# A decoder trunk on one core: gate products and first projection of the gated-delta stage in eight blocks, three weight pieces split before the stage, convolution rows loaded and turned before its norm

## The chip, the core and the metric

The kernel runs on one core of a Trainium2 chip. The metric is the device time of one execution in microseconds (us). Five engines work side by side, each with its own instruction queue: TensorE (PE, with PEld for its weight loads), VectorE (DVE), ScalarE (ACT), GpSimd (POOL) and SyncE (SP), which here only starts DMAs. They are ordered by semaphores alone: an instruction that waits holds up all that stands behind it on its engine.

## The reference

The program is one inference step of a four-layer decoder for 256 prompt tokens and 32 sample tokens (8 sequences of 4). Tokens lie side by side, so an activation is 1024 features by 288 tokens. Each layer is half an FFN, a token mixer and half an FFN, all behind an RMSNorm:

```
x = x + 1/2 * FFN_a(RMSNorm(x));  x = x + Mixer(RMSNorm(x));  x = x + 1/2 * FFN_b(RMSNorm(x))
```

The mixers of the layers are RWKV-7, differential attention, gated DeltaNet and RWKV-7. The change is in the entry of the gated DeltaNet (third layer):

```
proj = u @ p['w_in']                       # u = RMSNorm(x); 1024 -> 3072 (q|k|v) + 1024 (z) + 8 (b) + 8 (a)
xp = concatenate([conv_prev, qkv], axis=1) # 3 rows of state per sequence
conv = sum(p['conv_w'][j] * xp[:, j:j + T] for j in range(4))
qkv_c = silu(conv)
beta = sigmoid(b_raw);  g = -exp(a_log) * softplus(a_raw + dt_bias)
```

Then come l2 norms of q and k, a chunked delta rule in chunks of 64, a gated norm and the output projection.

## The kernel before

Twelve stages follow one another: ffn, rwkv, ffn, ffn, attn, ffn, ffn, **gdn**, ffn, ffn, rwkv, ffn. The residual `x` stays in SBUF as [128 partitions, 8 blocks of features, 288 tokens]. The order on every engine is written out by hand in five functions, one per engine, each with a loop over the stages.

**Weights.** SP streams all weights through `ring`, four slots of 2 MB (a "unit"). Unit N goes to slot N mod 4, and SP waits until unit N-4 is released (`wait_released`). The gdn stage `s` has `b = unit_base[s]` with the small gate weights (16 columns), units b+1 to b+8 with the 32 pieces of `w_in` (four pieces of 128 output columns each), and b+9, b+10 with the output weights.

**Split products.** Large products are made as three fp32r products (`three_products`, L965 to L967): weight and activation are each split into a high part (ACT casts it) and a low part (DVE subtracts it from the original). Low parts of gdn pieces go to `ring_lo`, which has the ring's layout; high parts go to three buffers `gdn_w_hi` that piece q shares with piece q+3. A piece is 8 blocks (k) of three products, 24 in all, into bank c mod 4.

**The FFN ahead of the stage.** Its last eight units are the down projection. PE makes 33 products for each of two halves (e = 0, 1) of a unit; the last two halves give blocks 6 and 7 of `x` (DVE, L3465). `half_done` counts finished halves and pieces; HD(u, n) is its value when n parts of unit u are done.

**Entry of the stage, before.** PE: `norm(s)` (three fp32 products of ones with the squares of blocks 5 to 7, into bank 0; GpSimd has added the others to them), three idle-time products `keep_clock` (L961), a wait for the DMA of `conv_rows` (24 state rows), 24 transposes of them (L1686), a wait for all eight normed blocks `h`, the gate products (L1695: 4 chunks x 8 blocks x 2 partition halves; L1699: 8 blocks x 4 row groups for the sample tokens), then pieces c = 0 to 31. GpSimd starts the DMA of `conv_rows` when all of `x` is updated (L3645, L3646). ACT: squares of blocks 6 and 7, the root of the mean (`root`, L2144, L2146), eight casts `h_hi` (L2494), and after `prev_ready` the high parts of pieces 0 to 2 (L2490). DVE: eight normed blocks (L2704), eight low parts (L3211), zeroings, two copies of the turned rows (L3218, `prev_ready`), low parts of pieces 0 to 2 (L3207), and small gate parameters.

**Behind it.** For piece c, ACT splits piece c+3 and copies the product out; DVE makes the convolution of c and the low part of c+3. At c = 3 both work on the gate logarithms, and PE makes the cumulated gates (`gate_sums`) behind piece 5.

Of the kernel before, what the change touches and what calls it, by code (L numbers as in the profile page):

```python
# [10 lines left out]
NT = SEQ + NS  # L11
# [131 lines left out]
def program(nc, t, stages):  # L143
# [5 lines left out]
    with ctx:  # L149
# [339 lines left out]

        def leads_to_split(s):  # L490

            return s + 1 < len(stages) and stages[s + 1][0] in ("ffn", "attn")
# [280 lines left out]

        conv_in = shift_in
# [70 lines left out]
        def _(sp):  # L845
# [25 lines left out]
            def wait_released(N):  # L871
# [55 lines left out]
        def _(pe):  # L927
# [752 lines left out]
            def gdn(s):  # L1680
                b = unit_base[s]
                base = proj_before[s]
                keep_clock(5, 3)
                after(conv_in, 16)
                for c in range(24):
                    last = nc.tensor.transpose(bank[6 + c // 12][:, 24 * (c % 12):24 * (c % 12) + 24],  # L1686
                                               conv_rows[:, 128 * c:128 * c + 128], ident[0:24, 0:24])
                last.then_inc(prev_raw, 1)
                pe.wait_ge(h_ready, 8 * (normed_before[s] + 1))
                unit_in(b)  # L1690
                w = ring[:, b % SLOTS, 0:128].rearrange("p (k n) -> p k n", n=16)
                for c in range(NCHUNK):
                    for k in range(CH):
                        for r in HALVES:
                            nc.tensor.matmul(bank[4][r, 16 * c:16 * c + 16], h[:, k, RC * c:RC * c + RC], w[:, k, :],  # L1695
                                             start=(k == 0), stop=(k == CH - 1))
                for k in range(CH):
                    for q, r in enumerate(ROWS):
                        last = nc.tensor.matmul(bank[4][r, 64:68], h[:, k, SEQ:], w[:, k, :].rearrange("p (w a q) -> p q w a", w=2, a=2)[:, q],  # L1699
                                                start=(k == 0), stop=(k == CH - 1))  # L1700
# [3 lines left out]
                for c in range(32):  # L1704
# [4 lines left out]
                    pe.wait_ge(split_lo, split_before[s] + CH + c + 1)  # L1709
                    w_hi_c, w_lo_c = gdn_w_hi[c % 3], out_piece(b + 1, c, True)  # L1710
# [335 lines left out]
            for s, (kind, n) in enumerate(stages):  # L2046
                if kind in ("rwkv", "gdn"):
                    norm(s)
# [57 lines left out]
        def _(act):  # L2106
# [88 lines left out]
            def high_part(u, e):  # L2195
# [4 lines left out]
                nc.scalar.copy(w_hi[e][:, 0:k, :], raw).then_inc(w_hi_ready, 1)  # L2200

# [279 lines left out]
            def gdn(s):  # L2481
                b = unit_base[s]

                def w_high(q):

                    if q % 4 == 0:
                        act.wait_ge(slot_full[(b + 1 + q // 4) % SLOTS], full(b + 1 + q // 4))
                    if q >= 3:
                        act.wait_ge(half_done, HD(b + 1 + (q - 3) // 4, (q - 3) % 4 + 1))
                    nc.scalar.copy(gdn_w_hi[q % 3][:, :, :], out_piece(b + 1, q)).then_inc(split_hi, 1)  # L2490

# [4 lines left out]
                for q in range(3):  # L2496
                    w_high(q)
# [26 lines left out]
                for c in range(24):  # L2524
                    act.wait_ge(half_done, HD(b + 1 + c // 4, c % 4 + 1))
                    w_high(c + 3)
# [29 lines left out]
                for d in range(CH):  # L2556
                    act.wait_ge(half_done, HD(b + 7 + d // 4, d % 4 + 1))
                    if d < 5:
                        w_high(27 + d)
# [124 lines left out]
        def _(dve):  # L2684
# [386 lines left out]

            def attention(s):
# [128 lines left out]
            def gdn(s):  # L3201
                b = unit_base[s]

                def w_low(q):

                    dve.wait_ge(split_hi, split_before[s] + CH + q + 1)
                    TT(out_piece(b + 1, q, True), out_piece(b + 1, q), gdn_w_hi[q % 3][:, :, :], ALU.subtract).then_inc(split_lo, 1)  # L3207

                for c in range(CH):
                    dve.wait_ge(split_hi, split_before[s] + c + 1)  # L3210
# [5 lines left out]
                after(prev_raw)  # L3216
                for i in range(2):
                    last = V.tensor_copy(conv_prev[:, 12 * i:12 * i + 12, :].rearrange("p c n -> p (c n)"), bank[6 + i][:, 0:288])  # L3218
                last.then_inc(prev_ready, 1)
                for q in range(3):  # L3220
                    w_low(q)
# [24 lines left out]
                for c in range(24):  # L3246
# [29 lines left out]
                    w_low(c + 3)  # L3276

                for j in range(16):
# [4 lines left out]
                    if j in (0, 5, 10, 15):  # L3283
                        w_low(27 + j // 5)
                w_low(31)
# [134 lines left out]
            for s, (kind, n) in enumerate(stages):  # L3420
# [3 lines left out]
                if kind == "gdn":  # L3424
                    norm(s, NORM + 8 * 7)
# [5 lines left out]
                if kind == "ffn":  # L3431
# [334 lines left out]
```

## Time and profile before

| what | value |
|---|---|
| three runs | 2860.9, 2862.41 and 2863.51 us; median 2862.41 |
| profiled execution | 2862.17 us, of which the span of the core's instructions is 2860.2 |
| PE busy | 2785.2 us, 97% of the span |
| DVE, ACT, POOL busy | 1690.4, 1223.5, 253.9 us |
| DMA | 402.73 MB, mean 141 GB/s |
| gdn stage | from about 1600 to 1900 us of the span |

Times in all views are us from the start of the span. "Idle before" is time in which an engine stood still ahead of an instruction, and the arrow names what released it. PE's rows count instructions as the hardware runs them: an fp32 product is two rows, an fp32r product one. The granted clock (PEclk) is 1.00 at 2.4 GHz and 0.50 at 1.2 GHz. DMA share is the busy share of the 16 DMA engines.

### The profile page before, as it was taken

What the parts mean: (1) busy time and instruction counts of PE and PEld (TensorE: products, weight loads), DVE (VectorE), ACT (ScalarE), POOL (GpSimd) and SP (SyncE); (2) the same over time, 40 slices, a digit from 0 to 9 for tenths busy, and PEclk for the clock granted to TensorE, in tenths of its full rate; (3) what the DMA queues carried; (4) which work ended last, traced back from release to release, by engine and by line L of the source; (5) the groups of instructions that cost most, each with busy time, mean ns of one, the idle gap of its engine ahead of it and who ended that gap; (6) DMA issues with size and microseconds to landing.
All of it is one profiled execution on the core that took longest, in us unless ns stands there. A gap on an engine that the chain in (4) does not pass through costs nothing.

```text
span 2860.2 us, 64280 instructions
## 1 busy us (share of the span) xinstructions
PE 2785.2 (97%) x28475; PEld 2615.8 (91%) x28475; DVE 1690.4 (59%) x2576; ACT 1223.5 (43%) x1921; POOL 253.9 (9%) x331
## 2 busy tenths in 40 slices
PE   7999999999999999999999999999999999999999
PEld 7997978899999986999999988789999979788999
DVE  5646865665565545665565574456556568756653
ACT  4434633544444334543443563234344346334433
POOL 1001011100000102000000111410000010111001
PEclk9999999999999999999999999999999999999999
DMA  7444410653644655444643443155464443205532
GB/s 247 158 138 137 130 38 4 197 160 129 204 152 138 242 178 196 148 148 138 198 158 123 152 146 97 52 167 164 138 193 154 142 146 118 61 4 156 173 131 77
DMA packets 349208, 402.73 MB, mean 141 GB/s; under 512 B 31210, under 2 KB 303999, under 8 KB 348573
## 3 DMA queue, kind: packets, MB, share of 16 engines
q1 hardware_dynamic: 338032, 361.76, 39.7%
q0 software_dynamic: 10976, 38.07, 4.4%
q8 instruction: 154, 2.52, 0.4%
q14 instruction: 46, 0.38, 0.0%
HBM read 385.22 MB, written 14.57 MB: 140 GB/s over the span
## 4 chain that ended last, share of the span: by engine, by line
PE 89%; DVE 7%; ACT 2%; issue 1%; DMA 1%; POOL 0%; SPq 0%; DVEq 0%; ACTq 0%; POOLq 0%
PE banks L965 24%; PE banks L967 23%; PE banks L966 23%; PE banks L1381 2%; PE banks L1353 1%; PE banks L1079 1%; PE banks L1046 1%; PE banks L1990 1%; DVE work L2935 1%; PE banks L1550 1%; PE banks L1462 1%; PE banks L955 1%; PE banks L1856 1%; PE banks L961 0%; DVE ring_lo L2794 0%
## 5 line engine op out<-in xcount | busy, mean ns | idle before, releaser
L2719 DVE TENSOR_TENSOR w_lo<-ring,w_hi 128x2048 fp32r<-128x2048 f32 (+1 forms) x304 | 611.4, 2012 | 412.2 <-ACT w_hi L2200 412.1
L965 PE MATMUL banks<-h_hi,w_hi 128*128 128x288 f32 x2816 | 837.9, 298 | 7.4 <-DVE h_lo L2711 7.0
L966 PE MATMUL banks<-h_hi,w_lo 128*128 128x288 f32 x2816 | 831.9, 295 | 0.0
L967 PE MATMUL banks<-h_lo,w_hi 128*128 128x288 f32 x2816 | 829.1, 294 | 0.0
L2200 ACT CAST w_hi<-ring 128x2048 fp32r<-128x2048 f32 (+1 forms) x304 | 511.3, 1682 | 576.7 <-PE banks L967 548.5
L965 PEld LDWEIGHTS banks<-h_hi,w_hi 128*128 128x128 f32 x2816 | 528.6, 188 | 10.6 <-issue 6.3
L967 PEld LDWEIGHTS banks<-h_lo,w_hi 128*128 128x128 f32 x2816 | 531.5, 189 | 0.0
L966 PEld LDWEIGHTS banks<-h_hi,w_lo 128*128 128x128 f32 x2816 | 529.8, 188 | 0.4
L965 PE MATMUL banks<-hid_hi,w_hi 128*128 128x288 f32 x1408 | 416.1, 296 | 0.0
L966 PE MATMUL banks<-hid_hi,w_lo 128*128 128x288 f32 x1408 | 415.4, 295 | 0.0
L967 PE MATMUL banks<-hid_lo,w_hi 128*128 128x288 f32 x1408 | 414.3, 294 | 0.0
L967 PEld LDWEIGHTS banks<-hid_lo,w_hi 128*128 128x128 f32 x1408 | 265.1, 188 | 0.0
L966 PEld LDWEIGHTS banks<-hid_hi,w_lo 128*128 128x128 f32 x1408 | 264.3, 188 | 0.0
L965 PEld LDWEIGHTS banks<-hid_hi,w_hi 128*128 128x128 f32 x1408 | 263.9, 187 | 0.0
L2664 ACT CAST hid_hi<-work 128x288 fp32r<-128x288 f32 x176 | 76.1, 433 | 398.4 <-DVE work L3453 398.4
L3506 POOL TENSOR_TENSOR h<-h 128x288 f32<-128x288 f32 x65 | 80.3, 1235 | 1713.9 <-ACT h L2153 912.4
L3446 DVE TENSOR_TENSOR work<-banks,rinv 128x288 f32<-128x288 f32 x176 | 80.6, 458 | 177.8 <-PE banks L967 177.8
L966 PE MATMUL banks<-h_hi,ring_lo 128*128 128x288 f32 x448 | 133.7, 298 | 0.0
L3455 DVE TENSOR_TENSOR hid_lo<-work,hid_hi 128x288 fp32r<-128x288 f32 x176 | 80.7, 458 | 87.8 <-ACT hid_hi L2664 87.8
L966 PEld LDWEIGHTS banks<-h_hi,ring_lo 128*128 128x128 f32 x448 | 85.9, 192 | 0.2
L2320 ACT COPY work<-banks 128x256 f32<-128x256 f32 x144 | 45.2, 382 | 89.9 <-PE banks L1381 84.7
L3465 DVE SCALAR_TENSOR_TENSOR x<-banks,x 128x288 f32<-128x288 f32 x64 | 29.3, 457 | 89.2 <-PE banks L967 89.2
(599 smaller groups left out, 4420.2 us busy)
## 6 DMA issues: line engine op xcount, KB each, us to landing
ring<-in_ffn_w_gate SPq DMA_DIRECT2D x88, 1024.0 KB, 5.4
ring<-in_ffn_w_up SPq DMA_DIRECT2D x88, 1024.0 KB, 7.9
ring<-in_ffn_w_down SPq DMA_DIRECT2D x64, 768.0 KB, 4.6
ring<-in_ffn_w_down SPq DMA_DIRECT2D x64, 640.0 KB, 5.8
ring<-in_rwkv_w_rkv SPq DMA_DIRECT2D x24, 1024.0 KB, 6.8
ring<-in_gdn_w_in SPq DMA_DIRECT2D x16, 1024.0 KB, 6.6
ring<-in_attn_w_qkv SPq DMA_DIRECT2D x12, 1024.0 KB, 7.5
ring<-in_rwkv_w_o SPq DMA_DIRECT2D x8, 1024.0 KB, 6.2
```

The costliest lines, as they stand in the source:

```text
L965: nc.tensor.matmul(out, w_hi_k, x_hi_k, start=start, stop=False)
L966: nc.tensor.matmul(out, w_lo_k, x_hi_k, start=False, stop=False)
L967: return nc.tensor.matmul(out, w_hi_k, x_lo_k, start=False, stop=stop)
L1381: last = nc.tensor.matmul(bank[(XT_BANK if w else XY_BANK)[g]][to, 64 * q:64 * q + 64], y if w else xt, xt if w else y, start=True, stop=True)
L2200: nc.scalar.copy(w_hi[e][:, 0:k, :], raw).then_inc(w_hi_ready, 1)
L2320: return nc.scalar.copy(dst[:, 4 * g:4 * g + 4], bank[banks_[g]][:, 0:256].rearrange("p (c n) -> p c n", n=64)).then_inc(ready, 1)
L2664: nc.scalar.copy(hid_hi[:, 2 * u + e, :], prod[:, e, :]).then_inc(act_hi_ready, 1)
L2719: nc.vector.tensor_tensor(w_lo[e][:, 0:k, :], raw, w_hi[e][:, 0:k, :], ALU.subtract).then_inc(w_lo_ready, 1)
L3446: nc.vector.tensor_tensor(silu[:, e, :], bank[2 * e][:, 0:NT], rinv[:, :], ALU.mult)
L3455: nc.vector.tensor_tensor(hid_lo[:, f, :], prod[:, e, :], hid_hi[:, f, :], ALU.subtract).then_inc(act_lo_ready, 1)
L3465: nc.vector.scalar_tensor_tensor(x[:, c, :], bank[4 + c % 4][:, 0:NT], 0.5, x[:, c, :], ALU.mult, ALU.add).then_inc(x_updated, 1)
L3506: nc.gpsimd.tensor_tensor(h[:, c, :], h[:, c, :], h[:, other, :], ALU.add).then_inc(presummed, 1)
```

## The change

1. **Convolution rows.** GpSimd starts their DMA (and the two small gate parameter DMAs behind it) at HD(unit_base[s]-1, 1), when the first half of the FFN's last unit is done, no longer at the last update of `x`. PE turns them ahead of `norm(s)`, into banks 1 and 2 in place of 6 and 7, and DVE copies them out ahead of its wait for the root.
2. **Three pieces ahead.** ACT casts pieces 0 to 2 ahead of its norm, into the unused part of slot b of `ring_lo` (`gdn_w_high`); DVE subtracts them in the FFN's last unit, between the updates of blocks 6 and 7 of `x`. Slot b is released only when three pieces of unit b+1 are done.
3. **Block by block.** PE makes the gate products of block k as soon as `h` block k is there, and behind them the three products of block k of piece 0. DVE alternates a normed block and a low part. Two `keep_clock` products stand where three stood. Piece 0 leaves the loop over c.

The order on the engines, with line numbers that differ from before because lines were added. First PE at the entry of the stage, before (L955 norm, L961 keep_clock, L1686 transposes, L1695 and L1699 gates, L965 to L967 piece 0):

```order
4516 L955 MATMUL banks<-h,consts 128x288 x3
4517 L961 MATMUL banks<-consts 128x512 x3
4518 L1686 MATMUL banks<-consts,work 128x24 x24
4519 L1695 MATMUL banks<-ring,h 64x16 x64
4520 L1699 MATMUL banks<-ring,h 32x4 x32
4521 L965 MATMUL banks<-h_hi,gdn_w_hi_79 128x288
4522 L966 MATMUL banks<-h_hi,ring_lo 128x288
4523 L967 MATMUL banks<-h_lo,gdn_w_hi_79 128x288
```

And PE at the same place now (L1697 transposes, L967 norm, L973 keep_clock, L1709 and L1712 gates of one block, L977 to L979 products of one block):

```order
4516 L1697 MATMUL banks<-consts,work 128x24 x24
4517 L967 MATMUL banks<-h,consts 128x288 x3
4518 L973 MATMUL banks<-consts 128x512 x2
4519 L1709 MATMUL banks<-ring,h 64x16 x8
4520 L1712 MATMUL banks<-ring,h 32x4 x4
4521 L977 MATMUL banks<-h_hi,ring_lo 128x288
4522 L978 MATMUL banks<-h_hi,ring_lo 128x288
4523 L979 MATMUL banks<-h_lo,ring_lo 128x288
4524 L1709 MATMUL banks<-ring,h 64x16 x8
4525 L1712 MATMUL banks<-ring,h 32x4 x4
```

The transposes moved ahead of the norm, and the gates were cut into eight groups with three products behind each. Second DVE from the last updates of `x` on, before (L3465 update of x, L2704 normed blocks, L3211 low parts of h, L3218 copy of turned rows, L3207 low part of a piece):

```order
1195 L3465 SCALAR_TENSOR_TENSOR x<-banks,x 128x288 x2
1196 L2704 SCALAR_TENSOR_TENSOR h<-x,prm,rinv 128x288 x8
1197 L3211 TENSOR_TENSOR h_lo<-h,h_hi 128x288 x8
1198 L3213 MEMSET work 128x3 x4
1199 L3214 MEMSET work 128x48
1200 L3215 MEMSET work 128x192
1201 L3218 COPY work<-banks 128x288 x2
1202 L3207 TENSOR_TENSOR ring_lo<-ring,gdn_w_hi_79 128x8x128
```

And DVE now (L3492 update, L3098 low parts of pieces, L3234 copy of turned rows, L2726 normed block, L3242 low part of h):

```order
1195 L3492 SCALAR_TENSOR_TENSOR x<-banks,x 128x288
1196 L3098 TENSOR_TENSOR ring_lo<-ring,ring_lo 128x8x128 x3
1197 L3492 SCALAR_TENSOR_TENSOR x<-banks,x 128x288
1198 L3234 COPY work<-banks 128x288 x2
1199 L2726 SCALAR_TENSOR_TENSOR h<-x,prm,rinv 128x288 x2
1200 L3242 TENSOR_TENSOR h_lo<-h,h_hi 128x288
1201 L2726 SCALAR_TENSOR_TENSOR h<-x,prm,rinv 128x288
1202 L3242 TENSOR_TENSOR h_lo<-h,h_hi 128x288
```

The three low parts now stand ahead of the last update of `x`, and the copy of the turned rows ahead of the normed blocks. The diff, cut to its core:

```diff
+        def gdn_w_high(s, q):
+            if q < 3:
+                return ring_lo[:, unit_base[s] % SLOTS, 1024 * (q + 1):1024 * (q + 2)].rearrange("p (k n) -> p k n", n=128)
+            return gdn_w_hi[q % 3]
...
@@ SP, wait_released(N)
-                if stages[owner][0] == "ffn":
+                if stages[owner][0] == "gdn" and N == unit_base[owner]:
+                    sp.wait_ge(half_done, HD(N + 1, 3))
+                elif stages[owner][0] == "ffn":
...
@@ PE, gdn(s)
-                keep_clock(5, 3)
                 after(conv_in, 16)
                 for c in range(24):
-                    last = nc.tensor.transpose(bank[6 + c // 12][...
+                    last = nc.tensor.transpose(bank[1 + c // 12][...
                 last.then_inc(prev_raw, 1)
-                pe.wait_ge(h_ready, 8 * (normed_before[s] + 1))
+                norm(s)
+                keep_clock(5, 2)
                 unit_in(b)
+                unit_in(b + 1)
-                for c in range(NCHUNK):
-                    for k in range(CH):
+                for k in range(CH):
+                    pe.wait_ge(h_ready, 8 * normed_before[s] + k + 1)
+                    for c in range(NCHUNK):
                         for r in HALVES:
                             nc.tensor.matmul(bank[4][r, 16 * c:16 * c + 16], h[:, k, RC * c:RC * c + RC], w[:, k, :],
-                                             start=(k == 0), stop=(k == CH - 1))
-                for k in range(CH):
+                                             start=(k == 0 and c == 0), stop=(k == CH - 1), skip_group_check=True)
...
+                    if k == CH - 1:
+                        last.then_inc(half_done, 1)
+                    pe.wait_ge(split_lo, split_before[s] + 3 + k + 1)
+                    last = three_products(bank[0][:, 0:NT], gdn_w_high(s, 0)[:, k, :], out_piece(b + 1, 0, True)[:, k, :],
+                                          h_hi[:, k, :], h_lo[:, k, :], k == 0, k == CH - 1)
                 last.then_inc(half_done, 1)
                 after(prev_ready)
-                for c in range(32):
+                for c in range(1, 32):
...
@@ ACT, loop over the stages
+                if kind == "gdn":
+                    for q in range(3):
+                        gdn_piece_high(s, q)
                 if kind in ("rwkv", "gdn"):
                     norm(s)
...
@@ DVE, gdn(s)
+                after(prev_raw)
+                for i in range(2):
+                    last = V.tensor_copy(conv_prev[...], bank[1 + i][:, 0:288])
+                last.then_inc(prev_ready, 1)
+                inverse_rms(s)
+                normed(0, NORM + 8 * 7)
                 for c in range(CH):
-                    dve.wait_ge(split_hi, split_before[s] + c + 1)
+                    if c + 1 < CH:
+                        normed(c + 1, NORM + 8 * 7)
+                    dve.wait_ge(split_hi, split_before[s] + 3 + c + 1)
                     TT(h_lo[:, c, :], h[:, c, :], h_hi[:, c, :], ALU.subtract).then_inc(split_lo, 1)
...
@@ DVE, ffn, last units, ahead of the update of x
+                            if u == FFN_UNITS - 1 and e == 1 and leads_to_gdn(s):
+                                for q in range(3):
+                                    gdn_piece_low(s + 1, q)
...
@@ GpSimd, gdn_loads(s)
-                pool.wait_ge(x_updated, 8 * (s + 1))
+                pool.wait_ge(half_done, HD(unit_base[s] - 1, 1))
```

## Rows read from the trace of the kernel before

**Rows 1.** The page: the chain that ended last, by engine.
```profile
PE 89%; DVE 7%; ACT 2%; issue 1%; DMA 1%; POOL 0%; SPq 0%; DVEq 0%; ACTq 0%; POOLq 0%
```

**Rows 2.** The chain of waits, 1600 to 1613: start, us, what.
```profile
1600.37 0.47 DVE x L3465
...
1601.43 3.97 DMA work<-in_state_gdn_conv
...
1605.44 1.67 PE banks L1686 x24
1607.11 5.03 PE banks L1695 x128
1612.14 0.97 PE banks L1699 x64
```

**Rows 3.** Timeline of PE: keep_clock; gates in two single us; end of piece 0.
```profile
1601.94 2.74 PE L961 MATMUL banks<-consts 128*128 128x512 f32 x6
...
1607.82 1.38 PE L1695 MATMUL banks<-ring,h 128*64 128x16 f32 x42
...
1609.74 1.44 PE L1695 MATMUL banks<-ring,h 128*64 128x16 f32 x23
...
1617.61 0.29 PE L967 MATMUL banks<-h_lo,gdn_w_hi 128*128 128x288 f32 x1
1617.74 0.29 PE L965 MATMUL banks<-h_hi,gdn_w_hi 128*128 128x288 f32 x1
```

**Rows 4.** Granted clock by stretch (PEclk is the third number from the end).
```profile
1606.00:1609.00 3.00, 3.00 (x86) 2.96 (x85) 3.00 (x9) 1.14 (x3) 0.00 (x0) 1.00 0.00 0
...
1610.00:1616.00 6.00, 6.00 (x117) 5.93 (x116) 4.81 (x10) 3.37 (x6) 0.00 (x0) 0.50 0.27 61
...
1634.00:1635.00 1.00, 0.62 (x6) 0.60 (x6) 0.95 (x4) 0.96 (x3) 0.00 (x0) 1.00 0.66 240
...
1637.00:1643.00 6.00, 5.37 (x22) 5.40 (x23) 5.79 (x11) 3.02 (x10) 2.25 (x4) 0.50 0.00 0
```

**Rows 5.** Timeline of DVE, 1590 to 1618.
```profile
1595.97 0.46 DVE L3465 SCALAR_TENSOR_TENSOR x<-banks,x 128x288 f32<-128x288 f32 x1 [1.37 <-PE banks L967]
...
1603.15 3.52 DVE L2704 SCALAR_TENSOR_TENSOR h<-x,prm,rinv 128x288 f32<-128x288 f32 x8 [2.33 <-ACT rinv L2146]
1606.59 3.03 DVE L3211 TENSOR_TENSOR h_lo<-h,h_hi 128x288 fp32r<-128x288 f32 x8
...
1611.71 3.50 DVE L3207 TENSOR_TENSOR ring_lo<-ring,gdn_w_hi 128x1024 fp32r<-128x1024 f32 x3 [1.11 <-ACT gdn_w_hi L2490]
```

**Rows 6.** Timeline of ACT, 1590 to 1626.
```profile
1591.57 1.37 ACT L2200 CAST w_hi<-ring 128x1408 fp32r<-128x1408 f32 x1 [3.01 <-PE banks L967]
...
1602.14 0.50 ACT L2144 ACTIVATE rms<-banks,eps_col 128x288 f32<-128x288 f32 x1 [0.84 <-PE banks L955]
...
1624.34 1.05 ACT L2490 CAST gdn_w_hi<-ring 128x1024 fp32r<-128x1024 f32 x1 [1.63 <-PE banks L967]
```

**Rows 7.** GpSimd's other state load, L3512: issues, and its time to landing.
```profile
L3512 POOL DMA_DIRECT2D work<-in_state_rwkv_shift x2: 538/542/545, 226.4 to 2309.7; - x2
...
DMA to landing us min/median/max: 5.3/5.4/5.4
```

**Rows 8.** Windows around the loads: DMA share and GB/s are the last two numbers.
```profile
228.00:229.00 1.00, 1.00 (x10) 1.00 (x9) 0.86 (x1) 0.00 (x0) 0.00 (x0) 1.00 1.06 408
...
1598.00:1602.00 4.00, 3.95 (x25) 3.28 (x24) 0.46 (x1) 0.65 (x2) 0.55 (x1) 1.00 1.03 391
```

**Rows 9.** DMA issues, 1540 to 1700: a small load of the same queue.
```profile
work<-in_gdn_a_log POOLq DMA_DIRECT2D x1, 4.0 KB, 3.1
```

**Rows 10.** Timeline of PE at 1665: an fp32 product between fp32r products.
```profile
1665.57 0.29 PE L967 MATMUL banks<-h_lo,gdn_w_hi 128*128 128x288 f32 x1
1665.79 0.66 PE L1723 MATMUL banks<-work,consts 128*16 128x288 f32 x2
1666.38 0.40 PE L965 MATMUL banks<-h_hi,gdn_w_hi 128*128 128x288 f32 x1
```

More of the change, by code:

```diff
@@ L488, in split_gain, with leads_to_gdn @@
             return NORM + 8 * (3 * (stages[s][1] // 2) + 2 * (stages[s][1] % 2))
+        def leads_to_gdn(s):
+            return s + 1 < len(stages) and stages[s + 1][0] == "gdn"
         def leads_to_split(s):
@@ L1708, in gdn @@
                         pe.wait_ge(proj_evac, base + c - 2)
-                    pe.wait_ge(split_lo, split_before[s] + CH + c + 1)
-                    w_hi_c, w_lo_c = gdn_w_hi[c % 3], out_piece(b + 1, c, True)
+                    pe.wait_ge(split_lo, split_before[s] + (0 if c < 3 else CH) + c + 1)
+                    w_hi_c, w_lo_c = gdn_w_high(s, c), out_piece(b + 1, c, True)
                     for k in range(CH):
@@ L2046, in _ @@
             for s, (kind, n) in enumerate(stages):
-                if kind in ("rwkv", "gdn"):
+                if kind == "rwkv":
                     norm(s)
@@ L2200, in high_part, with gdn_piece_high @@
                 nc.scalar.copy(w_hi[e][:, 0:k, :], raw).then_inc(w_hi_ready, 1)
+            def gdn_piece_high(s, q):
+                b = unit_base[s]
+                if q == 0:
+                    act.wait_ge(slot_full[b % SLOTS], full(b))
+                if q % 4 == 0:
+                    act.wait_ge(slot_full[(b + 1 + q // 4) % SLOTS], full(b + 1 + q // 4))
+                if q >= 3:
+                    act.wait_ge(half_done, HD(b + 1 + (q - 3) // 4, (q - 3) % 4 + 1))
+                nc.scalar.copy(gdn_w_high(s, q)[:, :, :], out_piece(b + 1, q)).then_inc(split_hi, 1)
             def rwkv(s, j):
@@ L2482, in gdn @@
                 b = unit_base[s]
[L2484 to L2490, printed above, removed]
                 for c in range(CH):
@@ L2495, in gdn @@
                 act.wait_ge(prev_ready, 1)
-                for q in range(3):
-                    w_high(q)
                 after(pads_zeroed)
@@ L3070, in in_w_low, with gdn_piece_low @@
                 TT(out_piece(unit, q, True), out_piece(unit, q), in_buffer(q)[:, :, :], ALU.subtract).then_inc(split_lo, 1)
+            def gdn_piece_low(s, q):
+                unit = unit_base[s] + 1
+                dve.wait_ge(split_hi, split_before[s] + (0 if q < 3 else CH) + q + 1)
+                TT(out_piece(unit, q, True), out_piece(unit, q), gdn_w_high(s, q)[:, :, :], ALU.subtract).then_inc(split_lo, 1)
             def attention(s):
@@ L3215, in gdn @@
                 V.memset(gcol[:, :, :, :], 0.0).then_inc(pads_zeroed, 1)
[L3216 to L3221, printed above, removed]
                 after(gpar_in, 32)
@@ L3275, in gdn @@
                                 last.then_inc(conv_done, 1)
-                    w_low(c + 3)
+                    gdn_piece_low(s, c + 3)
                 for j in range(16):
@@ L3283, in gdn @@
                     if j in (0, 5, 10, 15):
-                        w_low(27 + j // 5)
-                w_low(31)
+                        gdn_piece_low(s, 27 + j // 5)
+                gdn_piece_low(s, 31)
                 dve.wait_ge(tail_rows_ready, 2)
@@ L3424, in _ @@
                 if kind == "gdn":
-                    norm(s, NORM + 8 * 7)
                     gdn(s)
```

12 lines of the change are left out of this document (5 added, 7 removed).

## The prediction, made before the changed kernel ran

> **What bounds the kernel now.** I read the page first: TensorE carries 89% of the chain that ended last [rows 1], so a change pays only by what it takes from TensorE's line of work or from a wait in it. Then the chain of waits at the entry of the gdn stage [rows 2]: the last update of x ends at 1600.84, the load of the convolution rows starts at 1601.43 and lands at 1605.40, and only then come the 24 transposes (1.67 us), the gates (5.03 and 0.97 us) and piece 0. The timeline of TensorE [rows 3] shows the end of piece 0: its last product starts at 1617.61, and piece 1 starts at 1617.74. Last, the granted clock [rows 4]: 1.00 up to 1609, 0.50 from 1610 to 1616. So a good part of the gates and more than half of piece 0 ran at 1.2 GHz. What TensorE did before the clock fell was 0.8 us of waiting, transposes and narrow gate products. The second stretch at 0.50 (1637 to 1643) likewise follows waits and narrow sums (busy 0.62 in 1634 to 1635).
>
> All behind piece 0 hangs on its end: ScalarE's split of piece 5 starts at 1624.34, right behind piece 2 [rows 6], and from there the chain goes through ScalarE and VectorE. Pieces 1 and 2 keep their price (48 products of 0.133 us, from the distance of the two starts in rows 3, 6.4 us). So I compare one number, the moment when piece 1 can start: 1617.74 before.
>
> **The convolution rows.** The trigger moves from 1600.84 to the end of the first half of the last FFN unit, 1595.97 [rows 5]. From the old trigger to the old DMA issue it took 0.59 us, so the new issue is at 1596.56. An undisturbed load (3.97 us, rows 2) would land at 1600.5, as the FFN ends. But it is not undisturbed: from 1598 to 1602 a ring load moves 391 GB/s at a DMA share of 1.03 [rows 8]. The nearest row is GpSimd's other state load, issued at 226.4 into the same traffic (408 GB/s, share 1.06, rows 8): with 32 KB it takes 5.3 to 5.4 us [rows 7], where a 4 KB load of the same queue without traffic takes 3.1 [rows 9]. The convolution load is 0.9 us longer than that small one (3.97 less 3.1). I take 5.4 + 0.9 = 6.3, so 1602.9, between 1600.5 and about 1604.
>
> The issue now also stands beside three low parts on VectorE. The Trainium skill ("SBUF — State Buffer", "A bandwidth-pool intuition that's wrong (but worth ruling out)") says that GpSimd can't write descriptors while VectorE holds the port pair they share. By it the load would wait until the three low parts end at about 1600, and land at about 1604; it is the late end of the range, and no row here shows it.
>
> On TensorE the transposes now stand ahead of the norm, so the norm waits for the load too. Before, only the gates did. This is the edit that turns against the change. Transposes from 1602.9 to 1604.6. The three norm sums: a keep_clock instruction of 512 columns is 0.457 us (2.74 by 6, rows 3), so 288 columns take 0.26 and three sums of two instructions 1.5 us: 1606.1. The root then starts 0.2 us later, at 1606.3, where it started at 1602.14 [rows 6]: 4.2 us later.
>
> **The norm and the blocks.** From the root to the first normed block 1.01 us (1602.14 to 1603.15, rows 5 and 6), so 1607.3. Its low part needs the block (0.44, 3.52 by 8), the cast on ScalarE (0.43 and two handoffs of 0.1) and 0.38 (3.03 by 8): 1608.8 [rows 5]. Two keep_clock products (1.8 us) end by 1607.9 and hide there. One block on TensorE then costs:
> - 16 gate instructions, at 42 per us at full clock [rows 3]: 0.38
> - 8 sample gate instructions, 0.97 us for 64 at half clock [rows 2], so 0.06 to 0.12; I take 0.1
> - three products of 0.133: 0.40
> - going from fp32r to fp32 and back. At 1665 the fp32 product starts 0.22 after the last fp32r product instead of 0.13, and the next fp32r product 0.59 after it, where two instructions of 288 columns need 0.51; the first one then also runs longer (0.40 for 0.29) [rows 10]. Together 0.28, between 0.1 and 0.4.
>
> That is 1.16 a block. VectorE needs 0.44 + 0.38 = 0.82 a block, so TensorE bounds the loop. First products at 1608.8, 0.4 for them, seven blocks more at 1.16 (8.1): piece 1 can start at 1617.3, 0.4 us before the old 1617.74. What was removed (a 0.8 us wait, one keep_clock product, piece 0 at half clock, piece 0's wait behind all gates) is eaten by the late root and by eight switches of product kind.
>
> **The clock.** From 1600.3 to 1604.6 TensorE now waits 2.6 us and then only transposes: 4.3 us much like those before the fall of rows 4. I expect it to fall to 0.50 within that stretch or just behind it. Prices: transposes, norm sums and keep_clock take up to double: 1.7 + 1.5, and 0.9 by which the two keep_clock products would then reach into the first block. So between 0 and 4.1; I take 2.0, as the fall comes at some point inside. Result: 1619.3, 1.6 us after the old one.
>
> The skill ("TensorE: Matmul & The Clock Gate", "Part 4: PE-mode transpose") says that a transpose doesn't count as activity for the clock as a product does. By it the transposes do nothing for the clock, and the fall is surer; before, 24 of them ran at 1.00 while the fall came only after the gates, which does not contradict it.
>
> **The pieces ahead.** ScalarE is free at 1592.94 (1591.57 + 1.37, rows 6); three casts of 1.05 end at 1596.1, before its square of block 6. VectorE takes the low parts behind the update that ends at 1596.43: 3.50 us [rows 5], end 1599.95. The update of block 7 starts at 1600.37: hidden, with 0.4 us to spare. If a load or GpSimd delayed them by more, each us would go straight into the norm. The late release of slot b (behind piece 2 rather than the gates) concerns a unit used from piece 12 on, 30 us later, against a load of some 7: nothing. ScalarE's gate copies now stand between the last low part and the split of piece 3, 0.3 us that pieces 1 and 2 (6.4 us) cover. GpSimd has nothing else to do while it waits.
>
> **Sum.** 2862.17 of the profiled execution + 1.6 = 2863.8; it lies 0.2 below the median of the runs, so against that I forecast 2863.9. A measurement of this kernel can't tell less than about 0.2% (5.7 us) from no change; this is inside.
>
> **Rivals.**
> A. The load lands in time (1600.5 to 1601.5). The ring load has ended its burst at 1602, and small packets may slip between. Then the transposes end by 1602.2, the root starts at 1603.9, 1.8 later than before, the clock doesn't fall, and the loop ends at 1614.9: 2.8 us gained, 2859.4. Against it stand both loads of rows 7, which agree within 0.1 us. Chance 0.2.
> B. Slower: the clock falls inside the loop of blocks, or the low level of the entry lasts into it. Place: the eight blocks, narrow gates beside three dense products. At half clock the gates take 23 a us [rows 3], so 0.70, the products 0.72, with 0.1 and 0.28 that is 1.8 a block instead of 1.16; before, the clock came back only after 3 us of dense products, which the blocks don't offer. Six blocks of it cost 3.9, half-clock products of pieces 1 and 2 another 2 to 3. With the sum above +8, so 2870. It decides if 0.50 stands in the rows of three blocks or more. For it: gates alone did not keep 1.00 (rows 4). Against it: the products are 0.40 of 1.16 us, which gates alone had not. Chance 0.25.
> C. More than the entry goes: the second stretch at 0.50 (1637 to 1643 cost 3 us) shifts away or shrinks together with A, 2856. Against it, its waits hang on ScalarE's chain behind piece 2, which only shifts. Chance 0.07.
> The forecast itself, 2861 to 2866.5: chance 0.48.
>
> **How the numbers follow.** B reaches past 2868.1 in some three quarters of its cases: slower 0.2. C and the tail of A (switches at 0.1, 1.3 us more): faster 0.08. The rest, 0.72, is within 0.2%. The range that leaves out no more than 2 in 10 goes from A with its cheap switches to B: 2858 to 2870.
>
> **What would show it.** In the changed profile: transposes start at 1602.5 to 1603.5, released by the DMA of the convolution rows (A: before 1601.6); the root at 1605.5 or later; clock 0.50 somewhere in 1602 to 1609; starts of the first products of two blocks 1.1 to 1.2 us apart at clock 1.00 (B: 1.7 or more); the three low parts on VectorE end before 1600.4, and the last update of x starts where it did; piece 1 starts at 1617 to 1620; the distance from there to the end of the stage is as before. The forecast is wrong if the load lands at 1601 or earlier, if the blocks come 0.9 us apart, or if the stage behind piece 2 changes its length.

## The result, and the profile after

| | before | after |
|---|---|---|
| median of the runs | 2861.24 us (20 runs) | 2866.81 us (20 runs) |
| ratio of the two | | 1.0021, 95% interval 1.0015 to 1.0027 |
| profiled execution | 2862.17 (span 2860.2) | 2864.69 (span 2862.7) |
| start of the last update of x, start of piece 1 | 1600.37, 1617.74 | 1600.62, 1624.11 |
| entry: the distance of these two | 17.37 us | 23.49 us |

The change costs 0.21%, some 6 us. The forecast had +1.6 us, in the same direction, and its range (2858 to 2870) holds the measured time; the entry of the gdn stage, the place it named, is 6.1 us longer and not 1.6. At the entry the changed kernel's trace runs 0.25 us later (1600.62 for 1600.37), so I compare distances, above all the **entry** of the last row of the table. All times and mean clocks in the tables are of the usual, fast executions; one of the ten of e2 below, 3830.62 us at a mean clock of 0.654, is left out.

The chain of the changed kernel by engine reads as before, word for word [rows 1], but at the entry it goes through the load (start us, us, what; L1697 the transposes, L967 the norm sums, L973 keep_clock, L1709 and L1712 the gates, L977 to L979 the products), against [rows 2]:

```profile
1596.80 7.63 DMA work<-in_state_gdn_conv
1604.43 0.04 issue
1604.47 2.75 PE banks L1697 x24
1607.23 3.18 PE banks L967 x6
1610.40 3.13 PE banks L973 x4
1613.54 0.57 PE banks L1709 x16
1614.11 0.17 PE banks L1712 x8
1614.29 0.33 PE banks L977
1614.62 0.13 PE banks L978
1614.75 0.13 PE banks L979
1614.88 0.57 PE banks L1709 x16
```

The load was issued 4.6 us earlier than before and landed only 1.0 us earlier: it took 7.63 us for 3.97. SyncE had started the ring load of unit b+3, two loads of 1 MB, 1.9 and 1.5 us before it:

```profile
1594.88 0.92 SPq L897 DMA_DIRECT2D ring<-in_gdn_w_in  x2
```

On the chain there stand behind the load, one after another and nothing between, the transposes, the norm sums, keep_clock and the first block. From one block to the next it is 1.34 us: 0.57 for 16 gate instructions, 0.17 for the samples, 0.59 for three products with the switch.

The windows of the changed kernel (us; busy time and count of PE, PEld, DVE, ACT, POOL; granted clock; DMA share; GB/s), against [rows 4, 8]:

```profile
1596.00:1600.00 4.00, 4.00 (x32) 4.00 (x31) 3.77 (x4) 1.76 (x3) 1.66 (x3) 1.00 0.98 317
1600.00:1603.00 3.00, 0.59 (x5) 0.35 (x3) 0.54 (x2) 0.44 (x1) 0.00 (x0) 0.98 1.07 261
1603.00:1613.00 10.00, 8.53 (x34) 5.83 (x34) 2.31 (x6) 1.80 (x4) 0.00 (x0) 0.50 0.15 35
1613.00:1624.00 11.00, 11.00 (x217) 9.04 (x217) 6.50 (x26) 2.77 (x7) 0.00 (x0) 0.99 0.01 1
1644.00:1647.00 3.00, 2.95 (x12) 2.98 (x13) 2.89 (x6) 2.45 (x8) 1.55 (x3) 0.50 0.00 0
```

TensorE stands still from 1600.6 to 1604.5, and the clock is at 0.50 from 1603 to 1613: transposes, norm sums and keep_clock all run at 1.2 GHz. The eight blocks themselves run at 1.00. VectorE's and ScalarE's timelines (start us, us, engine line op, out<-in), against [rows 5, 6]:

```profile
1596.60 3.48 DVE L3098 TENSOR_TENSOR ring_lo<-ring,ring_lo 128x1024 fp32r<-128x1024 f32 x3
1600.62 0.46 DVE L3492 SCALAR_TENSOR_TENSOR x<-banks,x 128x288 f32<-128x288 f32 x1 [0.54 <-PE banks L979]
...
1611.45 0.95 DVE L2726 SCALAR_TENSOR_TENSOR h<-x,prm,rinv 128x288 f32<-128x288 f32 x2 [3.36 <-ACT rinv L2164]
```

```profile
1610.44 0.50 ACT L2162 ACTIVATE rms<-banks,eps_col 128x288 f32<-128x288 f32 x1 [8.88 <-PE banks L967]
...
1630.76 1.05 ACT L2229 CAST gdn_w_hi<-ring 128x1024 fp32r<-128x1024 f32 x1 [1.65 <-PE banks L979]
```

The pieces ahead are hidden as forecast: the last low part ends at 1600.08, 0.54 us before the last update. The root starts at 1610.44, where it waited 8.88 us; before it started at 1602.14. The split of piece 5 starts at 1630.76 for 1624.34: 6.4 us later, so nothing is won back up to there. The profiled execution is only 2.5 us longer because of stretches of low clock elsewhere. The second one of the stage lasts 3.4 us for 6.8, so the next update of x behind the stage starts 4.66 us later than in the old profile (2057.09 for 2052.43), where the one ahead of it started 0.25 later: 4.4 us for the whole stage, 6.1 for its entry. Behind the stage the old profile has a stretch of 6.8 us near 2466, and the new one has one of 3.4 near 2340 instead. The runs, which average over such stretches, say 6 us.

### The profile page after: what moved, and what is told of

Read it like the earlier page. It is cut to its first block, busy times and chain, and to the rows that moved or that the text cites. A ratio compares the mean times of both kernels' runs of the same rounds, so it can differ in the third digit from the quotient of the medians.

```text
span 2862.7 us, 64276 instructions
## 1 busy us (share of the span) xinstructions
PE 2785.9 (97%) x28473; PEld 2613.6 (91%) x28473; DVE 1692.1 (59%) x2576; ACT 1222.7 (43%) x1921; POOL 254.6 (9%) x331
## 4 chain that ended last, share of the span: by engine, by line
PE 89%; DVE 7%; ACT 2%; issue 1%; DMA 1%; POOL 0%; SPq 0%; DVEq 0%; ACTq 0%; POOLq 0%
PE banks L977 24%; PE banks L979 23%; PE banks L978 23%; PE banks L1393 2%; PE banks L1365 1%; PE banks L1091 1%; PE banks L1058 1%; PE banks L967 1%; PE banks L2008 1%; PE banks L973 1%; DVE work L2957 1%; PE banks L1562 1%; PE banks L1474 1%; PE banks L1874 1%; DVE ring_lo L2816 0%
## 5 line engine op out<-in xcount | busy, mean ns | idle before, releaser
L977 PE MATMUL banks<-h_hi,w_hi 128*128 128x288 f32 x2816 | 838.9, 298 | 7.1 <-DVE h_lo L2733 6.7
L979 PE MATMUL banks<-h_lo,w_hi 128*128 128x288 f32 x2816 | 830.4, 295 | 0.0
L977 PEld LDWEIGHTS banks<-h_hi,w_hi 128*128 128x128 f32 x2816 | 529.1, 188 | 10.3 <-issue 6.0
L979 PEld LDWEIGHTS banks<-h_lo,w_hi 128*128 128x128 f32 x2816 | 532.2, 189 | 0.0
L977 PE MATMUL banks<-hid_hi,w_hi 128*128 128x288 f32 x1408 | 416.6, 296 | 0.0
L979 PE MATMUL banks<-hid_lo,w_hi 128*128 128x288 f32 x1408 | 415.0, 295 | 0.0
L979 PEld LDWEIGHTS banks<-hid_lo,w_hi 128*128 128x128 f32 x1408 | 265.5, 189 | 0.0
L977 PEld LDWEIGHTS banks<-hid_hi,w_hi 128*128 128x128 f32 x1408 | 264.1, 188 | 0.0
L3492 DVE SCALAR_TENSOR_TENSOR x<-banks,x 128x288 f32<-128x288 f32 x64 | 29.3, 457 | 85.7 <-PE banks L979 85.7
```

The costliest lines, as they stand in the source:

```text
L977: nc.tensor.matmul(out, w_hi_k, x_hi_k, start=start, stop=False)
L979: return nc.tensor.matmul(out, w_hi_k, x_lo_k, start=False, stop=stop)
L3492: nc.vector.scalar_tensor_tensor(x[:, c, :], bank[4 + c % 4][:, 0:NT], 0.5, x[:, c, :], ALU.mult, ALU.add).then_inc(x_updated, 1)
```

## The experiments

Each has its entry from one profiled execution, the mean granted clock over its timed runs (0.9951 for the changed kernel, 0.9954 to 0.9958 for the old one), and the ratio to the kernel before, timed beside it. An entry is one sample: e6 below has 16.00 and 20.52 from one kernel. e5 was run once only, for its load.

| | entry us | mean clock | ratio, 95% interval |
|---|---|---|---|
| before | 17.37 | 0.9954 to 0.9958 | 1 |
| changed kernel | 23.49 | 0.9951 | 1.0021 (1.0015 to 1.0027) |
| e1 transposes behind the norm | 21.99 | 0.9941 | 1.0018 (1.0009 to 1.0027) |
| e9 keep_clock in the wait | 19.47 | 0.9965 | 1.0015 (1.0006 to 1.0025) |
| e4 gates, then piece 0 | 22.55 | 0.9947 | 1.0015 (1.0006 to 1.0024) |
| e6 ring waits for rows | 16.00 and 20.52 | 0.9960 | 0.9999 (0.9990 to 1.0009) |
| e2 rows with unit b | 15.03 | 0.9977 | 0.9981 (0.9971 to 0.9991) |
| e3 the same, norm first | 14.29 | 0.9964 | 0.9996 (0.9987 to 1.0005) |
| e7 the same, gates first | 15.92 | 0.9960 | 0.9993 (0.9985 to 1.0002) |
| e10 e2 in pairs of blocks | 14.14 | 0.9971 | 0.9982 (0.9973 to 0.9991) |
| e12 old order, rows early | 17.46 | 0.9951 | 1.0003 (0.9994 to 1.0012) |

**e1: the order of transposes and norm.**

```diff
+                norm(s)
+                keep_clock(5, 2)
                 after(conv_in, 16)
                 for c in range(24):
 ...
-                norm(s)
-                keep_clock(5, 2)
```

> The transposes stand behind the norm and the two keep_clock products again; all else is as in the changed kernel. I measure the entry from the start of the last update of x to the start of piece 1: 17.37 us before the change, 23.49 after it. My theory: most of the loss is the norm that waits for the convolution rows and the low clock that this wait brings. Then the root comes some 1.8 us after that update starts, as before, the rows land at about 1604.4, the transposes end at 1606.1, and eight blocks of 1.34 us end at 1616.8: entry 16.2 us, time 6 to 7 us below the changed kernel and about 1 us below the old one. Rival: the blocks themselves are the cost (eight switches of product kind, narrow gates beside them), whatever stands ahead of them. Then the entry stays above 20 us.

The root came on time, the transposes ended at 1606.1 as computed, and still the entry is 21.99, not 16.2. TensorE's timeline:

```profile
1604.45 1.67 PE L1699 MATMUL banks<-consts,work 24*128 24x24 f32 x24 [0.78 <-DMA work<-in_state_gdn_conv]
1606.05 0.65 PE L1709 MATMUL banks<-ring,h 128*64 128x16 f32 x16
...
1609.06 1.04 PE L1709 MATMUL banks<-ring,h 128*64 128x16 f32 x16
...
1611.27 1.04 PE L1709 MATMUL banks<-ring,h 128*64 128x16 f32 x16
```

The first two blocks start 1.35 us apart; the clock falls at 1608.3, in the second, from the third block on they are 2.21 us apart, at 0.50, and the clock comes back only in piece 1 (1625.4). This is rival B of the prediction, in another kernel. My forecast for e1 fell: the norm was on time and the loss stayed. Its rival (the blocks cost it, whatever stands ahead) met its number, above 20 us, but not its reason: the blocks are not dear by themselves, they are dear at half clock. So e1 shows that moving the norm is not enough; what the late norm costs by itself it does not show.

**e9: the clock alone.** One line, `keep_clock(1, 4)`, ahead of the wait for the rows.

> As the changed kernel, with four more keep_clock products ahead of the wait for the convolution rows, where TensorE otherwise stands still (1600.6 to 1604.5). This prices the clock alone: the rows still land at about 1604.4. Theory (the idle wait brings the low clock, which then costs in transposes, norm sums, keep_clock and the first blocks): the clock stays at 1.00, the transposes take 1.7 for 2.75 us, the norm sums 1.5 for 3.2, the first products start some 3 to 4 us earlier: entry 19.5 to 20.5 us for 23.49. Rival: the clock falls as before because the transposes and the norm sums lower it by themselves; the entry stays above 22.5 us.

```profile
1603.25 1.67 PE L1698 MATMUL banks<-consts,work 24*128 24x24 f32 x24 [0.29 <-DMA work<-in_state_gdn_conv]
1604.85 1.72 PE L967 MATMUL banks<-h,consts 128*128 128x288 f32 x6
1606.41 1.88 PE L973 MATMUL banks<-consts 128*128 128x512 f32 x4
```

```profile
1603.00:1619.00 16.00, 15.70 (x250) 12.53 (x251) 8.80 (x31) 4.63 (x12) 0.00 (x0) 1.00 0.04 12
```

With the wait filled, the same three groups take 1.67, 1.72 and 1.88 us (in the same view of the changed kernel 2.75, 3.25 and 3.34, at half clock), and the entry 19.47: the low clock cost the changed kernel 4.0 us in its profile. The ratio moved by less (1.0015), and its interval does not exclude either 0 or 4 us: the runs can't confirm the size.

**e4: the switches.** Gates of all eight blocks, then the products of all eight.

> As the changed kernel, but TensorE makes the gate instructions of all eight blocks first (still block by block behind the norm) and then piece 0 in one go, so there is one switch of product kind in place of eight. If a block of 1.34 us holds 0.59 us for products that take 0.40 in a row, the eight switches cost some 1.5 us, and with the gates paced by VectorE (0.82 us a block) 0.9 to 1.5 us of them come back: entry 22.0 to 22.6 us for 23.49. Rival: the time belongs to the narrow gate instructions themselves, the entry stays within 0.4 us of 23.49. Second rival, the clock: six us of gates without dense products lower it, piece 0 then takes up to 6.4 us for 3.2, and the entry gets 2 to 3 us longer.

Entry 22.55, inside the theory's range, but by two effects at once: the transposes here ran mostly at 1.00 (1.83 us), and the clock fell in the last gates:

```profile
1615.77 0.65 PE L1710 MATMUL banks<-ring,h 128*64 128x16 f32 x16
...
1617.39 1.04 PE L1710 MATMUL banks<-ring,h 128*64 128x16 f32 x16
```

Inconclusive for the size of a switch; e10 measures it.

**e5 and e6: why the load takes 7.6 us.** e5 moves the low parts on VectorE behind the last update. e6 leaves them and adds this to SyncE's list of ring loads:

```diff
                 wait_released(N - SLOTS)
+                for g, (kind, n) in enumerate(stages):
+                    if kind == "gdn" and N == unit_base[g] + 3:
+                        sp.wait_ge(conv_in, 16 * 2)
```

> As the changed kernel, but VectorE makes the three low parts behind the last update of x in place of beside the load of the convolution rows. In the changed kernel the rows land 7.6 us after GpSimd's issue, and nothing of them moves in the first 3.7 us, until VectorE's low parts end; with both engines free the load took 3.97 us before. Theory (GpSimd can't write the descriptors while VectorE's low parts run, the Trainium skill's rule of the shared port pair): now the first packet comes 1.1 to 1.5 us after the issue and the rows land 4.0 to 5.5 us after it. Rival (the load stands behind the ring loads in the DMA engines): the landing stays 7.3 to 7.8 us after the issue. The low parts themselves now delay the root by up to 3 us, so the entry is not to be read here.

> As the changed kernel, but the ring load of unit b+3 waits until the convolution rows and the first small load have landed, so that less ring traffic stands beside them; VectorE's low parts stay where they are. Theory (the low parts hold up the descriptors): first packet still 3.5 to 3.8 us after the issue, rows landed 7.0 to 7.8 us after it. Rival (ring traffic is the cause): first packet within 1.5 us, rows landed 4.0 to 4.6 us after the issue, and the entry 23.49 shrinks to about 21.

The chain of e5 and its VectorE:

```profile
1592.42 8.06 DMA work<-in_state_gdn_conv
```

```profile
1596.25 0.46 DVE L3491 SCALAR_TENSOR_TENSOR x<-banks,x 128x288 f32<-128x288 f32 x1 [3.94 <-PE banks L979]
1596.62 3.49 DVE L3098 TENSOR_TENSOR ring_lo<-ring,ring_lo 128x1024 fp32r<-128x1024 f32 x3
```

The chain of e6, its VectorE, and a window beside the load:

```profile
1595.64 3.98 DMA work<-in_state_gdn_conv
```

```profile
1595.45 3.49 DVE L3101 TENSOR_TENSOR ring_lo<-ring,ring_lo 128x1024 fp32r<-128x1024 f32 x3
```

```profile
1596.00:1600.00 4.00, 3.76 (x31) 3.53 (x30) 3.39 (x4) 1.33 (x3) 1.30 (x3) 1.00 0.34 76
```

With VectorE idle for the first 3.8 us after the issue the load still took 8.06; with VectorE busy over nearly the whole load, but no ring traffic, it took 3.98, as before the change [rows 2]. My theory (descriptors held up by VectorE) fell twice, the rival stands: the ring load of unit b+3, issued just ahead, is what the rows wait behind. The DMA records split the 3.65 us that it costs: the first packet of the rows moves 3.6 us after the issue (1.2 in e6), and from there to the landing it is 4.0 us (2.8 in e6), as the ring load is not done yet.

For the late end of the landing I had worked out about 1604 from the Trainium skill ("SBUF — State Buffer", "A bandwidth-pool intuition that's wrong (but worth ruling out)"), and the load landed there, but by luck and not for that reason. That passage measured its delay beside a `tensor_copy` on VectorE; the low parts here are TENSOR_TENSOR instructions, and beside them e6 shows no delay.

> The changed kernel with the one added wait (ring load of unit b+3 behind the convolution rows), timed against the kernel before. One look gave an entry of 16.00 us for 23.49 and no stretch at half clock in it. Theory (ring traffic beside the load is what turned the change into a loss): 7 us below the changed kernel, so 0.998 to 0.999 of the kernel before. Rival (the one look was lucky in its clock, or the later ring load makes pieces wait): 1.000 or above.

Ratio 0.9999, 0.22% below the changed kernel: the one wait takes the whole loss back. But it is no gain against the old kernel. The first profile (2855.8 us) was lucky in its clock; the second, with the load again on time (4.15 us), was not:

```profile
1600.23 1.67 PE L1700 MATMUL banks<-consts,work 24*128 24x24 f32 x24 [0.41 <-DMA work<-in_state_gdn_conv]
1601.82 2.18 PE L970 MATMUL banks<-h,consts 128*128 128x288 f32 x6
1603.79 3.17 PE L976 MATMUL banks<-consts 128*128 128x512 f32 x4
```

```profile
1603.00:1606.00 3.00, 3.00 (x6) 1.52 (x5) 0.95 (x2) 1.34 (x3) 0.00 (x0) 0.50 1.04 400
1606.00:1613.00 7.00, 7.00 (x134) 5.24 (x132) 6.72 (x26) 3.06 (x8) 0.00 (x0) 0.97 0.24 87
1613.00:1620.00 7.00, 7.00 (x91) 6.01 (x84) 0.31 (x2) 0.28 (x2) 0.00 (x0) 0.51 0.00 0
```

The same kernel had an entry of 16.00 at 1.00 throughout and one of 20.52 with two low stretches. What the clock does there differs from execution to execution, and the timed runs are a mean over such executions.

**e2, e3, e7, e10: the rows much earlier.** The rows come with the ring load of unit b into free columns of its slot, as four groups of 24 partitions:

```diff
+                state = t["state_gdn_conv"][0].rearrange("b j n -> (b j) n")
                 units.append(([(0, 128, 8, 2 * GH, src[:, 4 * D:].rearrange("(k q) n -> q k n", q=128))]
+                              + [(128, slice(32 * g, 32 * g + 24), 1, 768, state[:, 768 * g:768 * g + 768].unsqueeze(1)) for g in range(4)], 1))
```

e2 keeps the changed kernel's order, and its transposes wait until seven blocks of x are updated; e3 has norm, transposes, one keep_clock product; e7 is e3 with all gates ahead of piece 0; e10 is e2 with gates and products in pairs of blocks.

> The changed kernel's order (transposes, norm, two keep_clock products, blocks), but the convolution rows come with the ring load of unit b, long before the stage. This prices the late rows and all that follows from them. Theory: no wait, transposes of 0.9 us (as with the rows in four groups of partitions), norm sums at full clock, root 2.8 us after the start of the last update of x, first products at 5.4 us, eight blocks of 1.34: entry 16 us, 7.5 less than the changed kernel, of which some 4 are the clock (the run with keep_clock products in the wait gave 19.47) and 3.5 the rows. Rival: without the wait the clock falls later, in the blocks (2.21 us each there, as in the run with the transposes behind the norm), entry 19 to 21 us.

> The convolution rows come with the ring load of unit b, long before the stage, into free columns of its slot (four groups of 24 partitions), and the order on TensorE is norm, transposes, one keep_clock product, blocks. Theory (late rows and late norm are the loss, and the blocks cost 1.34 us each at full clock): the wait for the rows is gone, the transposes run from about 1602.2 to 1603.9 in the time of the root, the first low part is there at about 1604.9, and the entry takes 15.0 us, 2.4 less than before the change and 8.5 less than after it. Rival 1, the clock: without dense products TensorE's clock falls in the blocks, which then take up to 1.9 us, and the entry takes 18 to 20 us. Rival 2: the blocks are the loss, the entry stays above 20 us.

> Rows with unit b, order norm, transposes, one keep_clock product, then the gate instructions of all blocks and then piece 0. Against the run that differs only in the interleaving (entry 14.29): gates 0.75 us a block but paced by VectorE's 0.82, so 6.0 to 6.6, one switch, piece 0 in 3.2. Theory (a switch costs 0.19 us, seven fewer): entry 13.0 to 13.6 us and, if the clock stays at 1.00, the fastest of all, some 0.1% below the old kernel. Rival: eight blocks of gates without dense products bring the low clock at their end, as in the run with gates first, piece 0 takes up to 5.8 us, entry 15 to 17 us.

> Rows with unit b, transposes first, norm, two keep_clock products as in the fastest run so far (entry 15.03, 0.9981 of the kernel before), but gates of two blocks and then the products of the two: four switches of product kind for eight. Theory: 0.19 us for each of four switches less, entry 14.2 to 14.5 us, clock at 1.00, time equal to that run within what can be measured. Rival: fewer switches but longer runs of narrow gates, clock at 0.50 inside the blocks, entry above 16 us.

TensorE in e2, a window of it, then e10 and e7:

```profile
1599.71 1.00 PE L1705 MATMUL banks<-consts,ring 24*128 24x24 f32 x24
1600.64 1.72 PE L974 MATMUL banks<-h,consts 128*128 128x288 f32 x6
1602.20 1.88 PE L980 MATMUL banks<-consts 128*128 128x512 f32 x4
1604.07 0.65 PE L1717 MATMUL banks<-ring,h 128*64 128x16 f32 x16
```

```profile
1603.00:1615.00 12.00, 11.96 (x221) 9.53 (x220) 7.98 (x29) 4.25 (x12) 0.00 (x0) 1.00 0.01 1
```

```profile
1606.54 0.65 PE L1718 MATMUL banks<-ring,h 128*64 128x16 f32 x16
...
1609.03 0.65 PE L1718 MATMUL banks<-ring,h 128*64 128x16 f32 x16
```

```profile
1610.11 0.65 PE L1717 MATMUL banks<-ring,h 128*64 128x16 f32 x16
...
1610.86 1.01 PE L1717 MATMUL banks<-ring,h 128*64 128x16 f32 x16
```

e2 came out a little better than its theory (15.03 for 16) and is 0.19% faster than the kernel before, 0.4% faster than the changed one. Its runs have a mean clock of 0.9977: 0.0023 x 2860 x 2 = 13 us at half clock, where the old kernel's 0.9958, timed beside it, makes 24. A dense us at half clock loses half of itself, so these 11 us are worth at most 5.5, as much as the measured 0.19% (5.4 us). That is an upper bound: over the executions of one kernel 0.001 of mean clock goes with some 1.75 us (an estimate from 200 executions, each against the mean of its kernel), which gives 3.3 for these 0.0019. By these two figures the clock is some three fifths to all of e2's gain; the runs don't divide it further. e10 has 2.49 us for two blocks in place of 2.68, so a switch costs 0.19 us, and the entry is 0.9 shorter; the runs can't tell it from e2. In e7 the clock fell in the last gates (rival met: entry 15.92), in its timed runs it is no better than the old kernel within the interval. e3 has a shorter entry than e2 and the higher ratio (the two intervals just meet). Its runs have the lower mean clock (0.9964), but in its profiled entry it stayed at 1.00. The one profile has the low stretch near 1634 at 6.8 us, where e2 has 3.4, and another of 3.4 near 1897; whether that is the rule in its runs is open.

**e12: is the block order worth anything?** The old kernel with the early trigger and e6's wait, nothing else.

> The kernel before the change, with only two things altered: the convolution rows are loaded at the new, earlier trigger, and the ring load of unit b+3 waits for them. Norm, three keep_clock products, transposes, all gates, piece 0 stand in the old order. This asks what the block by block order is worth once the rows are there in time. Theory (at full clock the block order costs as much as the old one; what decides is the wait and the low clock): the old wait of 0.8 us goes and the clock stays up longer, entry 14.0 to 15.5 us for 17.37, as good as the changed order with rows in time (15.03 and 16.00), time 0.1 to 0.2% below the old kernel. Rival 1 (the block order is worth 2 us or more by itself): entry 16.5 us or more and more than 2 us above the run with the rows in unit b. Rival 2 (the gates in a row lower the clock whatever comes before): piece 0 at half clock, entry 16 to 17.4.

```profile
1608.39 4.69 PE L1698 MATMUL banks<-ring,h 128*64 128x16 f32 x128 [0.45 <-DVE h L2707]
1613.02 1.04 PE L1702 MATMUL banks<-ring,h 128*32 128x4 f32 x64
...
1614.75 0.58 PE L968 MATMUL banks<-h_hi,gdn_w_hi 128*128 128x288 f32 x1 [0.70 <-DVE ring_lo L3210]
```

```profile
1613.38 3.50 DVE L3210 TENSOR_TENSOR ring_lo<-ring,gdn_w_hi 128x1024 fp32r<-128x1024 f32 x3 [1.11 <-ACT gdn_w_hi L2493]
```

A window of e12 (the granted clock is the third number from the end):

```profile
1611.30:1618.00 6.70, 6.00 (x113) 5.91 (x110) 5.48 (x17) 3.37 (x6) 0.00 (x0) 0.50 0.41 113
```

Entry 17.46, ratio 1.0003: the numbers of rival 1, with the mechanism of rival 2 in them. Without the wait for the rows TensorE waits 0.45 us for the last normed block and 0.70 for the low part of piece 0, which VectorE makes only behind norm, low parts of h and copies. Then piece 0 runs mostly at half clock: 4.74 us (1614.75 to 1619.49) for the 3.2 of 24 products at full clock. Without these 1.5 us the entry would be some 15.9 (an estimate from this trace), as much as e6's 16.00, which has the new order, the same early load and the same wait, and no low clock. The timed runs of the two agree as well (1.0003 and 0.9999, intervals that overlap). So with the rows loaded in the same way, block order and pieces ahead show no gain over the old order. The 2.4 us to e2 (15.03) hold the clock, and the rows that come with unit b; the old order with those rows was not run, so what the order adds to e2's gain is open.

## Why the prediction was right, and where it was not

**Direction and mechanism: right.** The transposes ahead of the norm make the norm wait for the load, and what the change removes is eaten by that: e6, which only brings the rows in time, takes back 0.22%, and e2, which also turns them in four groups, 0.40%. The pieces ahead are hidden with 0.54 us to spare (0.4 forecast). Up to the split of piece 5 all behind piece 1 keeps its distance; the stage behind that is 1.7 us shorter in the profile, by the second low stretch, where I had it unchanged.

**Sizes: three terms too small.** The +1.6 us was under a third of what came. On the old kernel's scale (0.25 us less), in the order of the sum:
- The landing: 1604.2 for 1602.9. The 5.4 us of [rows 7] were the right row: that load too was issued behind two ring loads (SyncE's row below), and its first packet moved 4.0 us after the issue. What was too small is the 0.9 for the larger load, taken from loads without traffic: beside the rest of the ring load the rows need 4.0 us from first packet to landing, the 32 KB of [rows 7] 1.3 to 1.4.
- The clock: priced at 2.0 us, between 0 and 4.1; e9 puts it at 4.0, so the bound held and the middle did not. I had put the fall "inside the stretch"; it came at 1602.9, before the first transpose, so transposes (2.75 for 1.67), norm sums (3.18 for 1.5) and keep_clock (3.13, not hidden: it ended 0.6 us behind the first low part of h) all paid double. The root came at 1610.2 for 1606.3.
- A block: 1.34 us for 1.16, 1.3 us over the seven. The gates were misread: the "x42" of [rows 3] counts instructions that overlap that us, 1.38 us of work by the same row; 35 of them start in it, which gives 0.46 us for 16 and not 0.38. A group of 16 by itself takes 0.57. The switch was sized too high (0.28 for 0.19), the samples too low (0.1 for 0.17).
- The sum: piece 1 at 1619.3 forecast; with 1.3, 2.0 and 1.3 more it is 1623.9, as measured.

```profile
224.49 0.94 SPq L885 DMA_DIRECT2D ring<-in_rwkv_w_rkv  x2
226.36 0.54 POOL L3512 DMA_DIRECT2D work<-in_state_rwkv_shift  x1 [0.29 <-POOL h L3506]
```

Three of the signs that I had named were missed with them: the start of the transposes, the distance of two blocks, and the start of piece 1. The 4.0 us are what the low clock costs the changed kernel, not what it adds: the old kernel's own stretch lasts 6.8 us (from 1609.4), and its mean clock over the runs is only 0.0003 to 0.0007 higher. I had also held less than 0.2% for no measurable change; the interval of the runs, 1.0015 to 1.0027, leaves no doubt that the kernel is slower.

**Rivals.** A (load in time) did not happen; e6 shows what it gives, 0.9999 of the old kernel (0.9990 to 1.0009), which neither confirms nor excludes the 2.8 us that I priced. B (low clock in the loop of blocks) did not happen in the profiled execution, where the low level ended at 1613.1, 0.4 us before the first block. It did in e1 and in the second profile of e6, so it is a real state of this loop, and dearer than I had it: 2.21 us a block for 1.8. C: the second stretch shrank from 6.8 to 3.4 us, but beside a longer first one. That the median, 2866.8, lies within my range owes something to luck: it is just above the forecast's own case (2861 to 2866.5), and the range held it because it was drawn wide for B, which the profile does not show.

**The Trainium skill's rule on transposes** ("TensorE: Matmul & The Clock Gate", "Part 4: PE-mode transpose"): the fall came in the idle wait ahead of them, so this case can't show whether they count.

## What to carry to other kernels

A load that is triggered earlier may be there hardly earlier (here 4.6 us and 1.0 us) if it now stands behind a bulk load on the DMA engines: let the bulk load wait for it, or let the rows ride with an earlier one. Before an in-order engine is made to wait for it, ask what is queued behind: here the norm, and with it every engine. And price an idle TensorE at the wait plus what runs at half clock behind it; here the second (4.0 us) was as large as the first (3.9). Last, compare a new order with the old one under the same loads: it was e12 beside e6 that left no gain of the block order that the runs can tell.

## What the runs showed of the hardware

- A load of 288 KB from GpSimd's queue, issued 1.5 us behind the second of two ring loads of 1 MB, took 7.5 to 8.1 us (7.63, 8.06, and 7.51 in e4) against 3.97 to 4.15 when none was issued in the 6 us before it; in the DMA records of the changed kernel its first packet moves 3.6 us after the issue, in e6 1.2 us.
- 24 transposes of 24 rows took 1.67 us from one group of partitions into two banks, and 1.00 us from four groups into four banks (e2).
- One kernel, two executions, 4.5 us apart in the same piece of program (16.00 and 20.52 us), with loads that took 3.98 and 4.15 us: nearly all of it is the clock (e6). One profile does not price such a place.
